# ScalarE writes the first gates; one-hots written out; first splits inside the gate build; V splits between the halves of weighings

## The reference, cut to what matters

```python
def blk(tb):                                   # 128 tokens
    q = (tb @ wq).reshape(TOK_BLOCK, PEER_HEADS, 2, PEER_DK)
    s = jnp.einsum('thpd,hpkd->thpk', q, keys)
    sv, si = lax.top_k(s, PEER_TOPK)           # 16 best of 128 keys, twice per head
    cand = sv[:, :, 0, :, None] + sv[:, :, 1, None, :]
    fv, fi = lax.top_k(cand, PEER_TOPK)        # 16 best pairs per head
    eid = i1 * PEER_NKEYS + i2                 # expert number
    g = jax.nn.softmax(fv, axis=-1)
    hid = jax.nn.gelu(jnp.einsum('td,ted->te', tb, u_tab[eid]))
    return jnp.einsum('te,ted->td', g * hid, v_tab[eid])
```

## Time and profile before

| | us |
|---|---|
| median of 3 runs | 2331.97 |
| lowest, highest | 2328.59, 2339.39 |
| the profiled execution | 2328.66 |
| its span | 2326.9 |
| TensorE busy in the span | 2210.8 |
| VectorE busy | 1667.0 |
| ScalarE busy | 921.8 |
| GpSimd busy | 418.5 |

### The profile page before, as it was taken

How to read it: one execution, slowest core, us unless ns; L and a number is a source line. 1 busy time by engine, 2 the same in 40 slices (tenths; PEclk the granted TensorE clock), 3 DMA queues, 4 the chain that set the end, 5 groups by cost and what they waited for, 6 DMA issues and landing times.

```text
span 2326.9 us, 38919 instructions
## 1 busy us (share of the span) xinstructions
PE 2210.8 (95%) x14916; PEld 1947.7 (84%) x14916; DVE 1667.0 (72%) x3097; ACT 921.8 (40%) x1054; POOL 418.5 (18%) x363
## 2 busy tenths in 40 slices
PE   7899999779989999889999999999999999999996
PEld 2498889448969998889998889889888888988996
DVE  1269777434456799668887787888877888876686
ACT  1333232453353226444444344344343443444444
POOL 1043000300000019301122123222222222211000
PEclk9999999889999999999999999999999999999999
DMA  9978767967644554667899999998999999988863
GB/s 380 382 264 292 276 235 255 386 249 298 226 168 133 159 185 173 247 230 259 292 324 355 345 359 355 362 363 327 352 366 348 369 343 368 336 318 300 288 206 131
DMA packets 157365, 675.03 MB, mean 290 GB/s; under 512 B 17328, under 2 KB 17712, under 8 KB 134032
## 3 DMA queue, kind: packets, MB, share of 16 engines
q1 hardware_dynamic: 122112, 444.65, 54.0%
q0 software_dynamic: 33648, 219.49, 24.4%
q10 hardware_dynamic: 1440, 8.56, 0.9%
HBM read 650.68 MB, written 21.95 MB: 289 GB/s over the span
## 4 chain that ended last, share of the span: by engine, by line
PE 76%; DMA 9%; DVE 8%; POOL 3%; ACT 2%; issue 1%; SPq 0%; DVEq 0%; ACTq 0%
PE vb L1599 15%; PE zb L1584 14%; PE vb L1601 6%; PE zb L1586 6%; PE zb L529 6%; PE zb L531 5%; PE zb L530 5%; DMA raw<-in_v 3%; PE vb L1633 3%; PE vb L1623 3%; DMA ada_first<-in_w_ada 2%; POOL one L744 2%; PE vb L1229 2%; DVE lo L482 2%; PE zb L1229 1%
## 5 line engine op out<-in xcount | busy, mean ns | idle before, releaser
L473 ACT ACTIVATE hi<-raw 128x1024 fp32r<-128x1024 f32 x624 | 658.9, 1059 | 986.4 <-PE vb L1599 285.0
L482 DVE TENSOR_TENSOR lo<-raw,hi 128x1024 fp32r<-128x1024 f32 x624 | 762.7, 1226 | 294.6 <-ACT hi L473 286.0
L1584 PE MATMUL zb<-act_hl,hi 128*128 128x416 f32 x1792 | 558.0, 369 | 3.5 <-DVE lo L482 3.5
L1599 PE MATMUL vb<-w_rest,hi 128*128 128x416 f32 x1536 | 498.7, 369 | 0.0
L1586 PE MATMUL zb<-act_hl,lo 128*128 128x208 f32 x1680 | 436.0, 259 | 0.0
L1584 PEld LDWEIGHTS zb<-act_hl,hi 128*128 128x128 f32 x1792 | 335.8, 189 | 40.0 <-issue 28.9
L1601 PE MATMUL vb<-w_rest,lo 128*128 128x208 f32 x1280 | 331.0, 259 | 0.0
L1586 PEld LDWEIGHTS zb<-act_hl,lo 128*128 128x128 f32 x1680 | 321.2, 191 | 5.2
L1599 PEld LDWEIGHTS vb<-w_rest,hi 128*128 128x128 f32 x1536 | 290.6, 189 | 1.5
L529 PE MATMUL zb<-act_hl,hi 128*128 128x288 f32 x960 | 287.0, 299 | 0.0
L530 PE MATMUL zb<-act_hl,hi 128*128 128x288 f32 x960 | 282.5, 294 | 0.0
(11 more groups left out here) (291 smaller groups left out, 2806.3 us busy)
## 6 DMA issues: line engine op xcount, KB each, us to landing
raw<-in_v SPq DMA_DIRECT2D x256, 512.0 KB, 6.3
raw<-in_u SPq DMA_DIRECT2D x224, 512.0 KB, 6.0
raw<-in_w_in SPq DMA_DIRECT2D x80, 512.0 KB, 9.3
ada_first<-in_w_ada SPq DMA_DIRECT2D x64, 512.0 KB, 8.7
ada_mid<-in_w_ada SPq DMA_DIRECT2D x64, 512.0 KB, 5.5
ada_in<-in_w_ada SPq DMA_DIRECT2D x32, 512.0 KB, 8.9
raw<-in_w_out SPq DMA_DIRECT2D x32, 512.0 KB, 5.5
ada_last<-in_w_ada SPq DMA_DIRECT2D x32, 512.0 KB, 7.3
```

The lines of the kernel that those rows point to most:

```text
L473: act.activation(hi[s][:, :], raw[s][:, :], ACT.Copy).then_inc(hi_ready, 1)
L482: dve.tensor_tensor(lo[s][:, :], raw[s][:, :], hi[s][:, :].bitcast(F32), ALU.subtract) \
L1584: last = pe.matmul(zb[:, bank, 0:2 * ND], w_h, act_hl[:, k, :, 0:ND], start=(k == 0), stop=(k == KC - 1))
L1599: last = pe.matmul(vb[:, bank, 0:2 * ND], v_h, w[:, e % 2, :, :], start=(e == 0), stop=(e == GI - 1))
```

## The change

Four edits.

1. `G_first` becomes one tile, and ScalarE writes it straight from `vb`, one more instruction per group behind the copy to `stage`; GpSimd's copies and the semaphore `gates_kept` go, and who waited for it waits for `g_copied`.
2. VectorE's loop over pairs of groups is written out, so that addresses are constants.
3. The last four ahead units get four slots of their own, so `hi` and `lo` are free earlier: ScalarE's four splits of the first U quad stand behind blocks 8 to 11 of the build, one each. VectorE's four `lo` keep their place, directly behind the build, and no longer wait for the last four ahead units. SP's load of the first of these units also waits until the picks are copied, since the new slots lie where the top-k had its tiles.
4. The first V quad's splits stand between the halves of the weighings: weighing e, then split e - 1 of the V quad, then the second half of weighing e; on ScalarE the split before the rounding.

The diff, with context cut:

```diff
@@ -262,7 +262,8 @@
     gl_ahead = at("gl_ahead", [P, AHEAD, ND], F32, x_at)
-    ahead_in = [at(f"ahead_in{k}", [P, UNIT], F32, 16512 + 4 * UNIT * k) for k in range(12)]
+    ahead_in = [at(f"ahead_in{k}", [P, UNIT], F32,
+                   16512 + 4 * UNIT * k if k < 12 else peer + (24960, 29056, 59904, 89472)[k - 12]) for k in range(16)]
     ada_last = [at(f"ada_last{k}", [P, UNIT], F32, zone + (0 if k < 4 else 38400) + 4 * UNIT * k) for k in range(8)]
@@ -288,7 +289,7 @@
     stage = [at(f"stage{b}", [P, NK, TB], F32, peer + (51712, 16640)[b]) for b in range(2)]
-    G_first = [at(f"G_first{b}", [P, TBLKS, GI * TB], F32, peer + 76160 + 6656 * b) for b in range(2)]
+    G_first = at("G_first", [P, 2, TBLKS, GI * TB], F32, peer + 76160)
     Gb = [at(f"Gb{b}", [P, TBLKS, GI * TB], F32, x_at + 6656 * b) for b in range(2)]
@@ -330,7 +331,6 @@
         ahead_used = sem("ahead_used")
-        gates_kept = sem("gates_kept")
         ahead_gelu = sem("ahead_gelu")
@@ -446,6 +446,8 @@
+            if u >= 2 * AHEAD - 4:
+                return 12 + u % 4
             return u if u < 4 else (8 if (u - 4) % 8 < 4 else 4) + u % 4
@@ -476,7 +478,7 @@
             if isinstance(q, int) and q == Q_PEER:
-                dve.wait_ge(ahead_used, 2 * AHEAD - 4 + s + 1)
+                dve.wait_ge(ahead_used, 2 * AHEAD - 12 + s + 1)
             if isinstance(q, int) and q == Q_OUT:
@@ -617,6 +619,8 @@
                     sp.wait_ge(ahead_used, u - 7)
+                if u == 2 * AHEAD - 4:
+                    sp.wait_ge(picks_copied, 3 * 3)
                 sp.dma_start(ahead_in[k][:, :], u_d[u // 2][:, UNIT * (u % 2):UNIT * (u % 2 + 1)]) \
@@ -732,9 +736,6 @@
                     .then_inc(g2_out[blk % 2], 16)
-                for b in range(2):
-                    pool.tensor_copy(G_first[b][:, blk, :].rearrange("p (i t) -> p i t", t=TB),
-                                     stage[blk % 2][:, GI * b:GI * b + GI, :]).then_inc(gates_kept, 1)
@@ -750,7 +751,6 @@
             pool.wait_ge(ahead_used, 2 * AHEAD)
-            pool.wait_ge(gates_kept, 2 * TBLKS)
             pool.memset(acc[:, :, :, :], 0.0).then_inc(acc_zero, 1)
@@ -1087,13 +1087,15 @@
                     act.wait_ge(g2_out[b], 8 * blk - 8 * b)
-                    act.wait_ge(gates_kept, 2 * blk - 2)
                 for k in range(2):
                     out = stage[b][:, :, 8 * k:8 * k + 8].rearrange("p i t -> p t i")
-                    act.activation(out, rows, ACT.Copy).then_inc(g_copied, 1)
+                    act.activation(out, rows, ACT.Copy)
+                    kept = G_first[:, :, blk, :].rearrange("p b (i t) -> p b i t", t=TB)[:, :, :, 8 * k:8 * k + 8]
+                    act.activation(kept, rows[:, :, 0:2 * GI].rearrange("p t (b i) -> p b i t", b=2), ACT.Copy) \
+                        .then_inc(g_copied, 1)
                     if g in ahead_ends:
@@ -1101,6 +1103,8 @@
                 gate_block(blk, blk % 2, blk < 2)
+                if TBLKS - 5 <= blk < TBLKS - 1:
+                    split_hi(act, Q_PEER, blk - TBLKS + 5)
@@ -1159,10 +1163,11 @@
-            quad_hi(Q_PEER)
             for e in range(PP + 1):
+                if e:
+                    split_hi(act, Q_PEER + 1, e - 1)
                 round_w(e, e % PP, e // PP)
-            for c in range(1, 6):
+            for c in range(2, 6):
                 quad_hi(Q_PEER + c)
@@ -2157,16 +2162,15 @@
-            with dve.Fori(0, G_GROUPS // 2) as i:
-                for b in range(2):
-                    g = 2 * i + b
-                    dve.wait_ge(g_ready, g + 1)
-                    for t in range(8 - ON_POOL):
-                        dve.tensor_scalar(one1[b][:, t, :], iota, i1T[:, bass.ds(8 * g + t, 1)],
-                                          gT[:, bass.ds(8 * g + t, 1)], ALU.is_equal, ALU.mult)
-                    dve.tensor_tensor(one2[b][:, :, :], over(iota, 8),
-                                      i2T[:, bass.ds(8 * g, 8)].unsqueeze(2).to_broadcast([P, 8, NK]),
-                                      ALU.is_equal).then_inc(one_ready, 1)
+            for g in range(G_GROUPS):
+                b = g % 2
+                dve.wait_ge(g_ready, g + 1)
+                for t in range(8 - ON_POOL):
+                    c = 8 * g + t
+                    dve.tensor_scalar(one1[b][:, t, :], iota, i1T[:, c:c + 1], gT[:, c:c + 1], ALU.is_equal, ALU.mult)
+                dve.tensor_tensor(one2[b][:, :, :], over(iota, 8),
+                                  i2T[:, 8 * g:8 * g + 8].unsqueeze(2).to_broadcast([P, 8, NK]),
+                                  ALU.is_equal).then_inc(one_ready, 1)
@@ -2178,7 +2182,7 @@
                 if isinstance(e, int) and e < 2 * PP:
-                    values, gates = gl_ahead[:, 2 * e:2 * e + 2, :], G_first[par]
+                    values, gates = gl_ahead[:, 2 * e:2 * e + 2, :], G_first[:, par, :, :]
                     dve.wait_ge(ahead_gelu, 2 * e + 2)
@@ -2186,7 +2190,7 @@
                 if pp == 0 and gates_wait is None:
-                    dve.wait_ge(gates_kept, 2 * TBLKS - 1 + par)
+                    dve.wait_ge(g_copied, G_GROUPS + 2)
                 elif pp == 0:
@@ -2299,8 +2303,9 @@
                 weigh(e, e % PP, e // PP, None)
+                if e:
+                    split_lo(dve, Q_PEER + 1, e - 1)
                 weigh_lo(e, e % PP, e // PP)
-            quad_lo(Q_PEER + 1)
             dve.wait_ge(acc_zero, 1)
```

## The result

The changed kernel takes 2317.3 us, median of 7 runs (2312.28 to 2323.56), against 2333.6 for the kernel before on the same chip: ratio 0.9935, interval 0.9922 to 0.9949. Its profiled execution took 2312.28, the lowest of the seven, with a span of 2310.4. The forecast was 2316 from the median and 2313.2 from the profiled execution. It is faster by over 0.5%, with an interval that lies just beyond that bound.

A forecast was written before the change was run, and what follows sets the result against it. TensorE was taken as 76% of the chain, GpSimd alone in the build. Gains of 6.0 and 9.5 sum to 15.5: 2313.2 from the profiled 2328.66, 2316.5 from the median 2331.97; range 2309 to 2322.

The forecast's parts named there:

- the turn: Passage from the gate build into the expert loop, through V columns 0 to 3: 9.5 us gain taken.
- The copies leave GpSimd: Gate build: 26 copies leave GpSimd's chain, VectorE takes over, block 6.23 to 5.70; 6.0 us gain in all.
- TensorE's 5.57: Gate build: time TensorE needs per block with its share of ahead products, 5.57 us; as bound, 7.3 gain.
- One-hots written out: VectorE in the gate build: 182 address steps go but run beside the one-hots; no gain taken, at most 2.6.
- The kept copy: ScalarE's added write of G_first per group: 0.45 us, ends 0.3 and 1.0; hidden except one at the build's end.
- The rule I weighed from the Trainium skill: ScalarE's G_first copy: SBUF wants two hits per 16-byte line, PSUM lines hold 8 bytes; strided read slow, estimate 0.95.
- First splits inside the build: First U quad: TensorE starts at t + 2.6 instead of t + 4.5, t being group 25's end; idle 1.5, not 3.45.
- V splits between the weighings: First V quad: V starts 12.8 us after group 25's end, 0.6 idle; four columns end at 22.4 instead of 32.2.
- still starts as the last write-out lands, at t + 6.7: GpSimd's clearing of acc, timed from t, group 25's end: takes 5.66, done at t + 12.4, before column 0.
- The second rival: First V quad: four loads late beside the last two write-outs; V starts near t + 15.4, total gain 11.5, 2320.5; chance 0.13.
- What follows keeps its order and its own waits: Everything behind the first V columns: unchanged, so the whole 15.5 us shift should reach the end.
- The port: Gate build: VectorE's one2 slows GpSimd's one-hots, block up to 6.0, total gain 12.0 to 13.7, 2319; chance 0.15.

The follow-up runs named there:

- after: The changed kernel with all four edits, as profiled, against the kernel before: 2317.3 us median, ratio 0.9935; profiled execution 2312.28.
- the run with five one-hots: Changed kernel with one of VectorE's six one-hots per group left out from group 2 on: 2322.5 us, 2335.7 for the kernel before beside it.

## Why the prediction was right, step by step

The total was right, with two terms off that cancelled: the build gave 8.65 instead of 6.0, the turn 7.35 instead of 9.5, the sum 16.0 instead of 15.5. That the sum came so near is in part luck.

- **The copies leave GpSimd: right, mis-sized.** The block is 5.44, not 5.70, below the 5.57 forecast for TensorE too. VectorE takes over, but not alone, and its own 5.69 was too long. After's VectorE rows of one group:

```profile
912.24 1.77 DVE L2170 TENSOR_SCALAR one<-consts,i1T,gT 128x128 f32<-128x128 f32 x6
913.84 1.21 DVE L2171 TENSOR_TENSOR one<-consts,i2T 128x1024 f32<-128x1024 f32 x1
914.97 1.10 DVE L2170 TENSOR_SCALAR one<-consts,i1T,gT 128x128 f32<-128x128 f32 x4
```

  A group is 914.97 - 912.24 = 2.73, a block 5.46. The forecast took the end of the second `one2` as the end of the block, but the next one-hot starts 1.13 after the start of a `one2` that lasts 1.21: 0.08 too much. The rest, 0.15, lay in the block I read: a duration from a block in which GpSimd was late is no duration of VectorE alone. Its first six one-hots stand 1.75 ahead of their `one2` there and 1.60 in after; what lengthened them no run shows.

  TensorE's 5.57 has the first of these faults. After's TensorE rows of one block:

```profile
926.07 2.02 PE L1571 MATMUL vb<-one,one 128*128 128x128 f32 x16
...
928.99 1.95 PE L1571 MATMUL vb<-one,one 128*128 128x128 f32 x16
930.77 0.87 PE L1547 MATMUL zb<-hF,ahead_in 128*128 128x208 f32 x4
```

  The next group starts at 931.53, 0.76 after the four ahead products begin, whose row lasts 0.87. So a block is 5.46 here from start to start, without idle time, and with that 0.76 the rows of the kernel before give the same: 892.63 + 0.76 - 887.93 = 5.46. The chain that ended last agrees; from 880 to 892 it is TensorE alone:

```profile
by line: PE vb L1571 71.0%; PE zb L1547 29.4%
```

  TensorE and VectorE arrive at the same pace, and no run separates which of the two sets 5.44. The forecast's bound of 7.3 for the build was wrong by the same 0.11 a block: 5.46 gives 8.5, and 8.65 was measured.
- **One-hots written out: nothing.** Right, shown by the loop put back.
- **The kept copy: right in kind.** It took 0.31, not 0.45. The forecast counted 256 elements where the row has 128 (two expert groups of 8, 8 tokens):

```profile
L1097 ACT ACTIVATE G_first<-vb x26: 297/312/331, 867.2 to 935.4; 128x128 f32<-128x128 f32 x26
```

  By the stage copy's price per element 128 would take 0.24, and the gelu of 208 elements takes 0.34 in after, so the price of the steps of 512 bytes is 0.1 at most. The rule I weighed from the Trainium skill ("SBUF — State Buffer", "Specifications (TRN2)") gave an estimate of 0.95, which for 128 elements is 0.47; this trace's 0.31 is below that too.
- **First splits inside the build: right.** U at t + 2.4 (forecast 2.6), idle 1.33 (1.5), full clock. Undone, it costs 2.2 of start and 2.7 of clock.
- **V splits between the weighings: right at V's start, wrong behind it.** V at t + 12.87 after 0.61 (forecast 12.8 and 0.6). The step that failed is "still starts as the last write-out lands, at t + 6.7": I kept the write-out's landing while moving the V loads next to it. The second rival had these loads beside the write-outs, but asked only what the write-outs do to the loads; it was the other way about. The four columns end at t + 23.6, not 22.4. A further 1.25 is given back behind them, of which 0.85 are the waits before columns 8 and 9, made by loads of 6 to 10 us beside the gathers. "What follows keeps its order and its own waits" was too simple: the order stayed, but the transfers met other ones.
- **The rivals.** The port didn't keep GpSimd late, since its one-hots now meet a `one2` late and it has idle time to wait in; the run with five one-hots shows how near that was. V data was not late for the first quad: its four loads took 4.2 to 9.6, and ScalarE's splits waited for TensorE's U units instead. ScalarE has 11 of 59.88 us to spare.

## What to carry to other kernels

Price the engine that takes over from stretches in which the old bound was not holding it, and from start to start, not from start to end; do the same for the engine behind it, or less work on the first is counted as a gain that the second takes back. When loads are moved earlier, ask what already flies there and who waits for that: here a write-out of 4.5 us took 9.85, and a clearing that waited for it became late. A wait of over 3 us on TensorE cost about as much again in slow clock at U (2.2 and 2.7), so a step that removes it can be worth more than its length: look for the same pattern further on in the trace, which here brought half as much again. It is no fixed price, though, as the next section shows.

## What the runs showed of the hardware

- Leaving out one of VectorE's six one-hots in each group made the block longer (5.44 to 5.52), while GpSimd's four one-hots in a block went from 4.05 to 5.12. Less work on one engine can slow another.
- A GpSimd one-hot took 0.87 clear of VectorE's `one2`, 1.26 when begun 0.71 us into it and up to 1.9 when begun with it.
- A wait of 3.54 before U was followed by a granted clock of 0.77 over the next 13.2 us, waits of 1.33 and 0.61 by 1.00. At the second V quad waits of 3.42 or 3.43 were followed, over as long a stretch, by 0.76 in after, 0.87 with VectorE's loop put back and 0.96 with the first U splits late; what makes the difference no run shows.
- The same loads of V columns 8 to 11 took 9.2 us (median) beside two row gathers and a load of gates, and 4.5 without. A write-out of 1 MB took 9.85 when issued among the first V loads, and 4.4 to 4.5 when issued ahead of them.
- A copy out of PSUM in steps of 512 bytes took 0.31 for 128 elements on ScalarE.
